# One prompt attention stage, two edits: value products from half-precision parts, and the softmax weighting of all units on GpSimd

## What is computed

```
s = q . k / 8 - slope * dist          (per branch, masked causally)
p = softmax(s)
o = g0 * p_cmp @ v_cmp + g1 * p_slc @ v_slc + g2 * p_win @ v_win
```

## Time and profile before

| What | us |
|---|---|
| Median of 3 runs (2915.94 to 2918.55) | 2917.19 |
| The profiled execution, its own time | 2923.37 |
| Its span in the trace | 2921.7 |
| PE busy | 2741.7 (94%) |
| DVE busy | 1270.4 (43%) |
| ACT busy | 1150.8 (39%) |
| POOL busy | 352.8 (12%) |

### The profile page before, as it was taken

One profiled execution on the slowest core, in us unless ns is written; L12 is line 12 of the kernel. 1 busy time (PEld: TensorE's weight loads), 2 busy tenths in 40 slices (PEclk: granted clock), 3 DMA queues, 4 the chain that ended last, 5 costly groups with the idle time before them and its releaser, 6 DMA issues.

```text
span 2921.7 us, 47262 instructions
## 1 busy us (share of the span) xinstructions
PE 2741.7 (94%) x18103; PEld 1823.3 (62%) x18103; DVE 1270.4 (43%) x2097; ACT 1150.8 (39%) x1593; POOL 352.8 (12%) x530
## 2 busy tenths in 40 slices
PE   5888898997999998999999999899998999999997
PEld 3667666655555564666666666566665666666664
DVE  8254454324555636444444122532336444443123
ACT  4664654322666724444444111211124444443111
POOL 0320303323000000111111000011100111111000
PEclk9899999999999999999999999999999999999999
DMA  3222223363000031111111111111111111111111
GB/s 131 79 73 63 67 64 121 105 187 110 1 1 1 4 112 37 51 50 50 50 50 53 64 49 41 44 50 50 51 44 37 52 49 49 50 50 64 53 54 59
DMA packets 113483, 173.19 MB, mean 59 GB/s; under 512 B 16993, under 2 KB 83922, under 8 KB 112978
## 3 DMA queue, kind: packets, MB, share of 16 engines
q1 hardware_dynamic: 92610, 150.90, 16.1%
q0 software_dynamic: 3792, 12.58, 1.3%
q10 hardware_dynamic: 16960, 8.16, 1.0%
HBM read 161.47 MB, written 14.30 MB: 60 GB/s over the span
## 4 chain that ended last, share of the span: by engine, by line
PE 78%; DVE 8%; SPq 6%; ACT 4%; issue 3%; DMA 1%; ACTq 0%; DVEq 0%
PE PS L1726 61%; PE PS L2050 5%; PE PS L2064 2%; ACT xT L823 2%; SPq L534 2%; SPq L537 2%; DVE R L1184 2%; PE PS L1706 2%; PE PS L1759 1%; PE PS L2021 1%; PE PS L1827 1%; DVE hT L1189 1%; PE PS L2022 1%; SPq L464 1%; SPq L459 1%
## 5 line engine op out<-in xcount | busy, mean ns | idle before, releaser
L1726 PE MATMUL PS<-hT,R 128*128 128x344 f16 x10152 | 1487.3, 310 | 6.1 <-DVE R L510 4.9
L1726 PEld LDWEIGHTS PS<-hT,R 128*128 128x128 f16 x10152 | 992.4, 98 | 498.4 <-DVE R L510 3.3
L510 DVE SCALAR_TENSOR_TENSOR R<-W,R 128x1024 f16<-128x1024 f32 (+1 forms) x186 | 248.5, 1336 | 964.2 <-ACT R L504 963.7
L504 ACT ACTIVATE R<-W 128x1024 f16<-128x1024 f32 (+1 forms) x186 | 206.5, 1110 | 923.6 <-PE PS L1726 919.3
L1726 PE MATMUL PS<-R 128*128 128x344 f16 x3276 | 478.2, 309 | 0.0
L1726 PEld LDWEIGHTS PS<-R 128*128 128x128 f16 x3276 | 320.2, 98 | 157.6
L1622 DVE SCALAR_TENSOR_TENSOR R<-R 128x1024 f32<-128x1024 f32 x96 | 123.3, 1285 | 79.3 <-ACT R L1127 78.0
L2050 PE MATMUL PS<-R 128*64 128x256 f32 (+1 forms) x592 | 155.0, 391 | 1.1 <-ACT R L1023 0.9
L823 ACT ACTIVATE xT<-xT 64x1024 f32<-64x1024 f32 x64 | 124.8, 1950 | 57.2 <-DMA xT<-cmp_t 56.0
L723 POOL COPY R<-R 128x2 f32 x88 | 19.4, 220 | 1035.8 <-ACT R L1126 1035.8
L1624 DVE SCALAR_TENSOR_TENSOR R<-R 128x1024 f32<-128x1024 f32 x96 | 123.3, 1285 | 13.6 <-DVE R L1623 12.3
(11 more groups left out here) (290 smaller groups left out, 2551.7 us busy)
## 6 DMA issues: line engine op xcount, KB each, us to landing
W<-wk SPq DMA_DIRECT2D x154, 512.0 KB, 3.4
W<-wdn SPq DMA_DIRECT2D x32, 704.0 KB, 4.0
xT<-cmp_t SPq DMA_DIRECT2D x256, 64.0 KB, 1.9
xT<-x SPq DMA_DIRECT2D x16, 516.0 KB, 7.3
o_y<-hT SPq DMA_DIRECT2D x6, 688.0 KB, 3.5
o_win_s<-state_win POOLq DMA_DIRECT2D x1, 4088.0 KB, 24.0
R<-s_hgrn POOLq DMA_DIRECT2D x4, 512.0 KB, 5.5
o_hgrn_s<-R ACTq DMA_DIRECT2D x4, 512.0 KB, 3.2
```

The lines of the kernel that those rows point to most:

```text
L504: act.activation(to[:, n, 0, 0:width], W[:, n, 0:width], ACT.Copy, scale=UNIT).then_inc(wh_here, 1)
L510: dve.scalar_tensor_tensor(to[:, n, 1, 0:width], W[:, n, 0:width], UNIT, to[:, n, 0, 0:width], ALU.mult, ALU.subtract).then_inc(w_split, 1)
L1726: ins = pe.matmul(wide(u)[:, m, :], weights[half], src[:, other, m * TW:(m + 1) * TW], start=(first and half == other == 0), stop=(last an ...
```

## The change

- **Values in half-precision parts.** Ahead of the stage ACT rounds the values to half precision (`VP`, `VPC`, 6 instructions) and DVE takes what that leaves (6 instructions). High and low part of one value head stand side by side as one stationary block of 128 columns. The weights are split too: ACT's copy of a transposed group now writes the high half (half precision, scaled by 1024), and a new DVE step `low_part` writes what is left, from the PSUM bank and the high half. The bank is given back (`t_free`) by `low_part` and no longer by ACT. A value block then takes two half-precision products of 256 columns (one for each half of the weights), in place of one 32-bit product.
- **The sum of the heads.** The 128 output rows now hold two sums of 64, the values' high part and their low part. `heads_out` on ACT copies one to `OTHER`; a new DVE step `heads_sum` adds the other one to it, writes `mix` and gives bank 6 back (`pv_free`).
- **The weighting.** The three multiplications of `weighted` go to GpSimd, for all 64 units (`by_pool` is always true). PE's transposes wait for GpSimd (`pw_pool`).
- **The rows that GpSimd splits** (`mix_parts`) go behind units 28, 36, 44 and 52 of its weighting, one row each.

```diff
         SS = [reg(17080 + n * 1728, 1728) for n in range(4)] + [xf[:, n * 1728:(n + 1) * 1728] for n in range(2)]
-        PT = reg(23992, 4, 4 * P)
+        PRODUCT = 1024.0
+        OTHER = reg(26608, 2 * P)
...
+        PT = halves(reg(23992, 2048)).rearrange("p (t s n) -> p t s n", t=4, s=2)
+        VP = halves(reg(10320, 2048)).rearrange("p (c t g n) -> p c t g n", c=2, t=NC, g=2)
+        VPC = halves(reg(28736, P)).rearrange("p (g n) -> p g n", g=2)
...
             wait_full(pool, U_S + 7)
-            for k in range(HA):
+
+            def mix_parts(k):
                 pool.tensor_copy(H2[:, k, 0, :], mix[:, k, :]).then_inc(mix_hi, 1)
                 pool.wait_ge(mix_hi, k + 1)
                 pool.tensor_tensor(H2[:, k, 1, :], mix[:, k, :], H2[:, k, 0, :], ALU.subtract).then_inc(mix_a, 1)
+
+            for n in range(len(units)):
+                i = units[n][0]
+                if by_pool(n):
+                    pool.wait_ge(rg_here, n + 1)
+                    for c, cols in spans(i):
+                        part = SS[n % SCORES][:, cols]
+                        ins = pool.tensor_scalar(part, part, RG[:, n % SCORES, c:c + 1], None, ALU.mult)
+                    ins.then_inc(pw_pool, 1)
+                if n in (28, 36, 44, 52):
+                    mix_parts((n - 28) // 8)
...
+            act.wait_ge(kl_here, 12)
+            for g in range(2):
+                part = slice(64 * g, 64 * g + 64)
+                for c, values in enumerate((VSL, VWN)):
+                    act.activation(VP[:, c, :, g, part], values[:, :, part], ACT.Copy).then_inc(vh_here, 1)
+                act.activation(VPC[0:NCP, g, part], VCP[0:NCP, part], ACT.Copy).then_inc(vh_here, 1)
             wait_full(act, U_S + 6)
...
                 act.wait_ge(pv_full, m + 1)
-                act.activation(mix[rows, HA + j:HA + j + 2, i * P:(i + 1) * P],
-                               PS[rows, 6, 0:2 * P].rearrange("p (a b) -> p a b", b=P), ACT.Copy).then_inc(pv_free, 1)
+                act.activation(OTHER[rows], PS[other, 6, 0:2 * P], ACT.Copy, scale=1 / PRODUCT).then_inc(oth_here, 1)
...
-                    act.activation(PT[:, turn % TURNED, 0:cols], PS[:, TURN_BANKS[turn % 3], 0:cols], ACT.Copy
-                                   ).then_inc(t_free, 1)
+                    act.activation(PT[:, turn % TURNED, 0, 0:cols], PS[:, TURN_BANKS[turn % 3], 0:cols], ACT.Copy,
+                                   scale=PRODUCT).then_inc(th_here, 1)
...
+            def heads_sum(m):
...
+                dve.wait_ge(oth_here, m + 1)
+                dve.scalar_tensor_tensor(mix[rows, HA + j:HA + j + 2, i * P:(i + 1) * P],
+                                         PS[rows, 6, 0:2 * P].rearrange("p (a b) -> p a b", b=P), 1 / PRODUCT,
+                                         OTHER[rows].rearrange("p (a b) -> p a b", b=P), ALU.mult, ALU.add).then_inc(pv_free, 1)
+
+            def low_part(m, g):
...
+                dve.wait_ge(th_here, turn + 1)
+                dve.scalar_tensor_tensor(PT[:, turn % TURNED, 1, 0:cols], PS[:, TURN_BANKS[turn % 3], 0:cols], PRODUCT,
+                                         PT[:, turn % TURNED, 0, 0:cols], ALU.mult, ALU.subtract).then_inc(t_free, 1)
...
+                if by_pool(n):
+                    return
                 dve.wait_ge(rg_here, n + 1)
...
             for m in range(len(units) // 2):
+                if m:
+                    heads_sum(m - 1)
                 biased(2 * m + 3)
                 weighted(2 * m + 2)
-                biased(2 * m + 4)
-                weighted(2 * m + 3)
+                count = groups[units[2 * m][0]]
+                for g in range(count):
+                    if g == count // 2:
+                        biased(2 * m + 4)
+                    low_part(m, g)
+                    if g == count // 2:
+                        weighted(2 * m + 3)
+            heads_sum(len(units) // 2 - 1)
...
-                            v = (VSL if kind == "slc" else VWN)[:, t, rows]
-                        ins = pe.matmul(PS[rows, 6, 0:2 * P], v, p, start=(g == b == 0), stop=(2 * g + b == len(bl) - 1),
-                                        skip_group_check=True)
+                            v = VP[:, ("slc", "win").index(kind), t, half, :]
+                        out = PS[:, 6, 0:2 * P]
+                        pe.matmul(out, v, high, start=(g == b == 0), stop=False, skip_group_check=True)
+                        ins = pe.matmul(out, v, low, start=False, stop=(2 * g + b == len(bl) - 1), skip_group_check=True)
                     return ins
...
-                pe.wait_ge(pw_here, 2 * m + 2)
+                for n in (2 * m, 2 * m + 1):
+                    pe.wait_ge(pw_pool if by_pool(n) else pw_here, weigh_turn(n) + 1)
```

More of the change, by code:

```diff
@@ L443, in program, with by_pool, weigh_turn @@
         SCORES, TURNED = 6, 4
+        def by_pool(n):
+            return True
+        def weigh_turn(n):
+            return sum(by_pool(k) == by_pool(n) for k in range(n))
         TURN_BANKS = (4, 5, 7)
@@ L1461, in _ @@
                                                      ALU.mult, ALU.subtract).then_inc(ql_here, 1)
+                    dve.wait_ge(vh_here, 6)
+                    for g in range(2):
+                        part, to = slice(64 * g, 64 * g + 64), slice(64 - 64 * g, 128 - 64 * g)
+                        for c, values in enumerate((VSL, VWN)):
+                            dve.tensor_tensor(VP[:, c, :, g, to], values[:, :, part], VP[:, c, :, g, part], ALU.subtract
+                                              ).then_inc(vl_here, 1)
+                        dve.tensor_tensor(VPC[0:NCP, g, to], VCP[0:NCP, part], VPC[0:NCP, g, part], ALU.subtract
+                                          ).then_inc(vl_here, 1)
             wait_full(dve, U_S + 7)
@@ L1485, in biased @@
                 ins.then_inc(sc_free, 1)
+            def heads_sum(m):
+                i, j, half = units[2 * m]
+                rows = slice(64 * half, 64 * half + 64)
+                dve.wait_ge(oth_here, m + 1)
[3 more added lines that the diff above has]
+            def low_part(m, g):
+                i = units[2 * m][0]
+                turn = group_at[m] + g
+                cols = 2 * P * len(blocks(i)[2 * g:2 * g + 2])
+                dve.wait_ge(th_here, turn + 1)
+                dve.scalar_tensor_tensor(PT[:, turn % TURNED, 1, 0:cols], PS[:, TURN_BANKS[turn % 3], 0:cols], PRODUCT,
+                                         PT[:, turn % TURNED, 0, 0:cols], ALU.mult, ALU.subtract).then_inc(t_free, 1)
             def weighted(n):
@@ L2036, in second @@
                 bl = blocks(i)
-                rows = slice(64 * half, 64 * half + 64)
                 def values(g):
@@ L2043, in values @@
                         pe.wait_ge(pv_free, m)
+                    if g == m == 0:
+                        pe.wait_ge(vl_here, 6)
                     for b, (kind, t, _) in enumerate(bl[2 * g:2 * g + 2]):
-                        p = PT[:, turn % TURNED, 2 * b * P:2 * (b + 1) * P]
+                        high, low = (PT[:, turn % TURNED, n, 2 * b * P:2 * (b + 1) * P] for n in range(2))
                         if kind == "cmp":
-                            v, p = VCP[0:NCP, rows], p[0:NCP]
+                            v, high, low = VPC[0:NCP, half, :], high[0:NCP], low[0:NCP]
                         else:
-                            v = (VSL if kind == "slc" else VWN)[:, t, rows]
-                        ins = pe.matmul(PS[rows, 6, 0:2 * P], v, p, start=(g == b == 0), stop=(2 * g + b == len(bl) - 1),
-                                        skip_group_check=True)
-                    return ins
-                pe.wait_ge(pw_here, 2 * m + 2)
+                            v = VP[:, ("slc", "win").index(kind), t, half, :]
+                        out = PS[:, 6, 0:2 * P]
+                        pe.matmul(out, v, high, start=(g == b == 0), stop=False, skip_group_check=True)
+                        ins = pe.matmul(out, v, low, start=False, stop=(2 * g + b == len(bl) - 1), skip_group_check=True)
+                    return ins
+                for n in (2 * m, 2 * m + 1):
+                    pe.wait_ge(pw_pool if by_pool(n) else pw_here, weigh_turn(n) + 1)
                 for g in range(groups[i]):
```

6 lines of the change are left out of this document (added).

## The result

The changed kernel takes 2930.37 us (median of 6 runs, 2927.39 to 2934.75) against 2917.95 for the kernel before (6 runs, 2915.94 to 2919.55): a ratio of 1.0044, 95% interval 1.0031 to 1.0057. It is slower by 12.4 us; forecast were 2906 and 11 us of gain, with 2888 to 2922 as the range. In the two profiled executions the attention stage is 13.8 us longer and the rest of the span 3.0 us shorter.

What follows compares the result with a forecast made beforehand. DVE was to set the pace in place of PE. Pairs -10.5, start -4.5 and row splits +4 sum to -11 us: 2912 for an execution like the profiled one, 2906 for the median, range 2888 to 2922.

Steps and rivals of the forecast that it cites:

- I take 1.0 (one tensor comes in), 1.75 us for the largest unit: GpSimd's multiplication by one number a row: 1.0 ns a column, priced from a one-input step, 1.041 us for 1032 columns.
- a rival's price: GpSimd's weighting at the two-input rate, 2.1 ns a column: 6 us, hence 2912 us; chance 0.10.
- it fits between `weighted` and the next pair's transposes for every i but 0: GpSimd's weighting, at 1.75 us for the largest unit, fits ahead of PE's next transposes except at i = 0.
- Rival 4: GpSimd becomes the bound at 3.1 ns a column, PE's transposes wait: 2946 us; 0.11, shared with dearer waits.
- Periods of 12.6, 11.85 and 11.0 us at i = 7 to 5: Time of one pair in the attention stage, from DVE's work plus two waits; all pairs together gain 10.5 us.
- Low parts 0.62 apart, PE's products 0.11 apart: DVE's `low_part` for 512 columns, 0.62 us start to start; PE's half-precision product of 256 columns, 0.11 us.
- Two waits a pair on DVE; the turn: DVE waits for scores mid-pair, 1.0 us at i = 7, and between pairs for ACT's heads, 2.1 to 1.1 us.
- rival 1: The turn between pairs costs less, ACT's copies running ahead of DVE's low parts: saves 17 us, 2889 us; chance 0.13.
- The start, 4.5 us earlier: At the stage's start, without GpSimd's row splits there, first transposes come at 728.6, 4.5 us earlier.
- The row splits, 4 us: GpSimd's splits in their new places hold DVE's gate product: nothing at i = 4, 1.2, 1.2, 1.8 at i = 3, 2, 1.
- A granted clock of 0.50 nowhere, "PE's pauses of 2 us are well short of the 5.90": PE's clock inside the stage would not fall to 0.50, seen after a pause of 5.90 us; such a fall would show error.

Runs made afterwards that it cites:

- run 5: Changed kernel, but GpSimd weights only the first 9 of every 32 columns, so the output is not the reference's: 2907.98 us, ratio 0.9963.
- run 3: Changed kernel with GpSimd's weighting as a product of two tensors, one the row's number repeated: 2914.42 us, ratio 0.9992.
- run 1: Changed kernel with all weighting back on DVE, so the value parts alone: 2970.28 us, ratio 1.0185.
- run 9: Changed kernel with only the scores of unit 2m+4 issued one group earlier on PE: 2922.10 us, ratio 1.0011.
- run 11: Run 8 with DVE's next `biased` put ahead of `heads_sum`: 2890.49 us, ratio 0.9913.
- run 8: Run 7 with PE issuing the scores of unit 2m+4 one group earlier, ahead of the value products: 2886.89 us, ratio 0.9893.
- run 6: Changed kernel with the four row splits behind units 3, 7, 11, 15 instead of 28, 36, 44, 52: 2934.62 us, ratio 1.0047.
- run 7: Changed kernel with the two-tensor product of run 3 and the early row splits of run 6: 2906.26 us, ratio 0.9955.
- run 10: Run 7 with eight idle products of 256 columns in PE's pause in each pair of i = 7 and 6: 2905.47 us, ratio 0.9947.

## Why the prediction was wrong

The step that failed is **"I take 1.0 (one tensor comes in), 1.75 us for the largest unit"** in the paragraph on GpSimd. The largest unit takes 5.14 us. The row it was taken from is a conversion to half precision; in the changed kernel the multiplication by one number costs 2.5 ns a column, more than the two-input step of 2.15 us for 1032 columns, which had been kept as a rival's price. With it fell "it fits between `weighted` and the next pair's transposes for every i but 0". Near the assumed price (run 5) 22.8 of the 24.9 us by which the stage missed are gone; with an operation that costs 1894 ns for 1024 columns in place of 2841 and computes the same (run 3), 15 us of the time are, by the ratios. The Trainium skill, GPSIMD Engine Reference, section Engine selection, gives one-input work on GpSimd as roughly line rate. The measurement differs (1882 against DVE's 549 ns for the same 640 columns) and decides; its advice to use VectorE would have been right about the price. But run 1 shows that on DVE it would cost this kernel still more.

Rival 4 had the mechanism, transposes that wait for GpSimd, and the point from which it decides (2.2 ns). Its time, 2946, was for 3.1 ns, and it was given 0.11. The choice between the prices was made by the number of inputs; the rows held no multiplication by one number on GpSimd at all, so nothing tied it to the cheapest of three.

By the prediction's other steps:
- *Periods of 12.6, 11.85 and 11.0 us at i = 7 to 5*: measured 12.6, 12.0 and 11.2. The working behind them holds: at i = 6 DVE waits 8.0 us in the turns, as forecast, and 4.1 in the middle of the pairs (forecast 3.6), and run 9, which takes the second wait away, wins 4.0. That the number held is partly luck. Near the price that the prediction assumed, three of the four pairs of i = 6 lost clock (run 5) and i = 7 and 6 took 52.0 and 51.1 us in place of 50.3 and 47.4. At the real price GpSimd's wait stood ahead of the one for the low part, PE's pause came in two pieces, and the clock was at 1.00 from 735.45 us on.
- *Low parts 0.62 apart, PE's products 0.11 apart*: right; three low parts take 1.88 us, hence 0.60 apart, and 256 columns 0.11, as before.
- *Two waits a pair on DVE; the turn*: 42.2 us of waiting for the heads are there, 1.9 and 2.0 a pair at i = 7 and 6, nearly as forecast, and less than forecast behind them. The 1.0 and 0.9 us a pair that rival 1 would save there were not seen. That a turn with less waiting would shorten the stage is not borne out by run 11, on run 8's order of issue; on the changed kernel's own order it was not tried.
- *The start, 4.5 us earlier*: at the predicted price it came 2.8 earlier (15.4 against 18.2). At the real price GpSimd takes 10.3 us for the two units that the first transposes need, and nothing is left of it.
- *The row splits, 4 us*: too little; moving them away gives 8.7 us back at i = 4 to 0 (run 6). DVE's gate product was held as said, though at other places: 1.32 at i = 4, where nothing was expected, 1.57 and 2.00 at i = 2 and 1, where 1.2 and 1.8 were; at i = 3, where 1.2 was expected too, no gate product met the split. The last one ends with GpSimd's step (timelines of the changed kernel), as the earlier trace rows had it. The rest is GpSimd's own 3.2 us for each split, which stand in its queue where the ring goes through it:

```profile
1000.22 2.00 DVE L1564 TENSOR_TENSOR R<-R 128x3 f32<-128x3 f32 x1
...
1000.06 2.14 POOL L730 TENSOR_TENSOR hT<-R,hT 128x1032 f16<-128x1032 f32 x1
```

- *A granted clock of 0.50 nowhere, "PE's pauses of 2 us are well short of the 5.90"*: wrong. Pauses of 1.76 to 2.28 us, one in each pair, went with a granted clock between 0.84 and 0.93 in runs 3, 5 and 7, with stretches at 0.50 (754.90 to 758.32 us in run 3), and the changed kernel has 0.80 at i = 2 to 0, where the one before had 1.00. At i = 6 it is shown to be what made runs 3, 5 and 7 slower, by the pairs that lost it beside the one that did not, and by run 10. For i = 2 to 0 it is argued from that.
